# The weighted sum over the index heads of the sparse attention layer, on TensorE instead of VectorE

## The reference, cut to what matters

```
k_sel = min(TOPK_MAX, S // 4)                    # 128
dots  = einsum('bqhd,bsd->bqhs', qib, ki)        # 8 heads, 64 wide
score = einsum('bqh,bqhs->bqs', wib, relu(dots)) * IDX_DIM ** -0.5
score = where(causal, score, -inf)
_, idx = lax.top_k(score, k_sel)
```

## Time and profile before

| | |
|---|---|
| median of 3 runs | 2972.53 us (2969.16 to 2978.28) |
| the profiled execution | 2973.47 us, its span 2971.7 us |
| busy share of the span | PE 93%, DVE 54%, ACT 39% |
| index heads, from ACT's first relu to the end of the last mask | 2258.87 to 2277.71 us of the span |
| in those 18.84 us | DVE busy 15.92, PE 15.63 (with overlaps), ACT 14.02 |

### The profile page before, as it was taken

The page is one execution under the profiler, slowest core; times in us unless marked ns, Lnnn a source line. Parts: engine busy times, 40 slices in busy tenths (PEclk is TensorE's granted clock), DMA queues, the critical chain, the costliest instruction groups (busy, mean ns, idle before and its releaser), DMA issues.

```text
span 2971.7 us, 39600 instructions
## 1 busy us (share of the span) xinstructions
PE 2760.0 (93%) x15280; PEld 2328.7 (78%) x15280; DVE 1596.2 (54%) x3415; ACT 1155.1 (39%) x2524; POOL 32.0 (1%) x32
## 2 busy tenths in 40 slices
PE   7998999999999899999998989999997689899998
PEld 7888889899888787878776767888775467688886
DVE  5354656555535555555578454444566845534445
ACT  3334332433333532343334543333346354432333
POOL 1000000000000000000000000000000000000000
PEclk9998999999999999999999999999998799999999
DMA  3201212122220111212221122332221011233322
GB/s 126 77 26 41 65 37 79 54 68 87 79 75 26 59 54 48 81 57 94 89 79 47 40 68 87 97 99 93 85 71 38 20 33 43 67 100 98 100 90 89
DMA packets 115260, 205.32 MB, mean 69 GB/s; under 512 B 13824, under 2 KB 23680, under 8 KB 114944
## 3 DMA queue, kind: packets, MB, share of 16 engines
q1 hardware_dynamic: 113920, 198.60, 21.6%
q10 hardware_dynamic: 1152, 4.20, 0.4%
HBM read 200.58 MB, written 2.10 MB: 68 GB/s over the span
## 4 chain that ended last, share of the span: by engine, by line
PE 74%; DVE 15%; ACT 8%; issue 2%; DMA 0%; SPq 0%; DVEq 0%; ACTq 0%
PE pp L1985 19%; PE pp L1987 18%; PE pp L1986 18%; PE pp L2059 5%; PE pp L2035 4%; DVE wl L1552 3%; PE pp L2047 2%; ACT wh L1371 2%; PE pp L1981 1%; PE pp L1982 1%; PE pp L1983 1%; ACT P L1481 1%; DVE P L1775 1%; DVE Z L1912 1%; DVE st L1910 1%
## 5 line engine op out<-in xcount | busy, mean ns | idle before, releaser
L1985 PE MATMUL pp<-Hh,wh 128*128 128x512 f32 (+1 forms) x2304 | 866.4, 376 | 75.0 <-DVE Hl L1574 29.4
L1986 PE MATMUL pp<-Hl,wh 128*128 128x512 f32 (+1 forms) x2304 | 802.2, 348 | 0.0
L1987 PE MATMUL pp<-Hh,wl 128*128 128x512 f32 (+1 forms) x2304 | 801.2, 348 | 0.0
L1552 DVE TENSOR_TENSOR wl<-raw,wh 128x512 fp32r<-128x512 f32 (+2 forms) x774 | 499.7, 669 | 419.5 <-ACT wh L1371 405.9
L1371 ACT ACTIVATE wh<-raw 128x512 fp32r<-128x512 f32 (+2 forms) x774 | 450.7, 604 | 328.8 <-PE pp L1987 274.9
L1985 PEld LDWEIGHTS pp<-Hh,wh 128*128 128x128 f32 x2304 | 448.1, 194 | 164.1 <-DVE wl L1552 36.2
L1986 PEld LDWEIGHTS pp<-Hl,wh 128*128 128x128 f32 x2304 | 448.4, 195 | 53.8 <-issue 6.5
L1987 PEld LDWEIGHTS pp<-Hh,wl 128*128 128x128 f32 x2304 | 446.8, 194 | 52.7
L1985 PE MATMUL pp<-Yh,wh 128*128 128x512 f32 (+1 forms) x1254 | 471.8, 376 | 10.9 <-DVE Yl L1572 5.7
L1987 PE MATMUL pp<-Yh,wl 128*128 128x512 f32 (+1 forms) x1254 | 449.4, 358 | 0.0
L1986 PE MATMUL pp<-Yl,wh 128*128 128x512 f32 (+1 forms) x1254 | 449.3, 358 | 0.0
(11 more groups left out here) (242 smaller groups left out, 2632.2 us busy)
## 6 DMA issues: line engine op xcount, KB each, us to landing
raw<-in_w SPq DMA_DIRECT2D x698, 256.0 KB, 2.6
raw<-in_w SPq DMA_DIRECT2D x36, 192.0 KB, 2.3
raw<-in_w SPq DMA_DIRECT2D x40, 128.0 KB, 2.0
out<-X SPq DMA_DIRECT2D x8, 256.0 KB, 2.0
con<-in_con ACTq DMA_DIRECT2D x1, 1576.0 KB, 11.5
X<-in_x SPq DMA_DIRECT2D x2, 528.0 KB, 5.8
X<-in_x ACTq DMA_DIRECT2D x2, 528.0 KB, 6.9
Z<-in_p ACTq DMA_DIRECT2D x2, 512.0 KB, 3.3
```

The costliest lines, as they stand in the source:

```text
L1552: e.tensor_tensor(part("wl", j), landing(j), part("wh", j).bitcast(F), ALU.subtract).then_inc(*dve.up("split", j))
L1985: e.matmul(it.ps, wh, xh, start=it.first, stop=False)
L1986: e.matmul(it.ps, wh, xl, start=False, stop=False)
L1987: e.matmul(it.ps, wl, xh, start=False, stop=it.end).then_inc(*pe.up())
```

## The change

The sum over heads leaves DVE. DVE first spreads four weights at a time on diagonals: `diagonals` multiplies the 128 x 128 identity, repeated four times, by four columns of `k2`, which gives four 128 x 128 diagonal matrices side by side. There are six such instructions (24 weight columns), into three buffers in `PT` and `P`. TensorE then multiplies the relu of each head by that head's diagonal matrix, all eight heads of a block accumulating in one bank (bank 6 for i = 1 and 3, bank 5 for i = 2), in float32. DVE reads the bank once per block, adding the mask (`index total`).

The order on TensorE: heads 0, 1, 2 of the index products first, then alternately the sum of head n and the index product of head n + 3, through all 24 heads, and three sums at the end. While this runs the rotation hands out six banks (0, 1, 2, 3, 4, 7). ACT's relu now waits for TensorE's `index sum` of three heads ago where it waited for DVE.

```diff
-        relus = []
+        diagonals = [m["PT"][:, 0:512], m["PT"][:, 640:1152], m["P"][:, 0:512]]
+        spread, summed, products = {}, {}, []
+        def diagonal(n):
+            i, h = 1 + n // 2, 4 * (n % 2)
+            spread[n] = do("diagonals", to=diagonals[n % 3].rearrange("p (h d) -> p h d", h=4), ident=ident, w=k2[:, i, h:h + 4],
+                           given=summed[n - 3] if n > 2 else None, begun=indexed)["n"]
+        def add_up(i, h, bk):
+            n, x = 2 * (i - 1) + h // 4, len(products)
+            products.append((i, h))
+            ext = 128 * i + 128
+            do("index sum", ps=bank(bk)[:, 0:ext], weights=diagonals[n % 3][:, 128 * (h % 4):128 * (h % 4) + 128], spread=spread[n],
+               rl=rl[x % 3][:, 0:ext], i=i, h=h, free=free[bk] if h == 0 else None)
+            if h % 4 == 3:
+                summed[n] = (i, h)
+            if h == 7:
+                do("index total", ps=bank(bk)[:, 0:ext], i=i, mask=causal(ext), score=sel[:, i, 0:ext])
+                free[bk] = ("dve", "index total", i)
+        for n in range(3):
+            diagonal(n)
+        held.add(6)
+        rot["banks"] = [0, 1, 2, 3, 4, 7]
+        relus, wanted = [], []
         for i in range(1, 4):
             ext = 128 * i + 128
             for h in range(8):
                 bk = next_bank()
...
                 relus.append((i, h))
                 free[bk] = ("act", "index", i, h)
-            do("index_mask", score=sel[:, i, 0:ext], mask=causal(ext))
+                wanted.append((i, h, 6 if i % 2 else 5))
+                if len(wanted) > 2:
+                    add_up(*wanted.pop(0))
+                    if len(products) in (4, 8, 12):
+                        diagonal(2 + len(products) // 4)
+        for each in wanted:
+            add_up(*each)
+        held.remove(6)
+        rot["banks"] = FREE
...
     # ScalarE, index
-            act.wait_ge("dve", "index", *it.taken)
+            act.wait_ge("pe", "index sum", *it.taken)
...
     # VectorE
-    def index(it): ...
-    def index_mask(it): ...
+    def diagonals(it):
+        for other in ("act", "pe"):
+            dve.wait_ge(other, "mark", it.begun)
+        dve.wait_ge("dve")
+        if it.given:
+            dve.wait_ge("pe", "index sum", *it.given)
+        e.tensor_tensor(it.to, it.ident.unsqueeze(1).to_broadcast([128, 4, 128]), it.w.unsqueeze(2).to_broadcast([128, 4, 128]), ALU.mult)...
+    def index_total(it):
+        dve.wait_ge("pe", "index sum", it.i, 7)
+        e.tensor_tensor(it.score, it.ps, it.mask, ALU.add)...
...
     # TensorE
+    def index_sum(it):
+        if it.free:
+            pe.wait_ge(*it.free)
+        pe.wait_ge("dve", "diagonals", it.spread)
+        pe.wait_ge("act", "index", it.i, it.h)
+        e.matmul(it.ps, it.weights, it.rl, start=it.h == 0, stop=it.h == 7)...
```

More of the change, by code:

```diff
@@ L1214, in mixer_c @@
                 do("index", i=i, h=h, ps=bank(bk)[:, 0:ext], q=M[64 * (h % 2):64 * (h % 2) + 64, h, 128 * i:ext], k=(twin if h % 2 else ki)[:, 0:ext], rl=rl[n % 3][:, 0:ext], free=free[bk],
-                   indexed=indexed, taken=relus[n - 3] if n > 2 else None, scale=k2[:, i, h:h + 1], score=sel[:, i, 0:ext])
+                   indexed=indexed, taken=relus[n - 3] if n > 2 else None)
                 relus.append((i, h))
                 free[bk] = ("act", "index", i, h)
-            do("index_mask", score=sel[:, i, 0:ext], mask=causal(ext))
+                wanted.append((i, h, 6 if i % 2 else 5))
[7 more added lines that the diff above has]
+        rot["banks"] = FREE
         def rounds(i):
@@ L1892, in query_scales @@
         e.tensor_scalar(it.col[:, 0:4], it.col[:, 0:4], -it.scale, None, ALU.mult).then_inc(*dve.up())
-    def index(it):
-        dve.wait_ge("act", "index", it.i, it.h)
+    def diagonals(it):
+        for other in ("act", "pe"):
+            dve.wait_ge(other, "mark", it.begun)
         dve.wait_ge("dve")
[L1897 to L1906, removed]
+        if it.given:
+            dve.wait_ge("pe", "index sum", *it.given)
+        e.tensor_tensor(it.to, it.ident.unsqueeze(1).to_broadcast([128, 4, 128]), it.w.unsqueeze(2).to_broadcast([128, 4, 128]), ALU.mult).then_inc(
+            *dve.up("diagonals", it.n))
+    def index_total(it):
+        dve.wait_ge("pe", "index sum", it.i, 7)
+        e.tensor_tensor(it.score, it.ps, it.mask, ALU.add).then_inc(*dve.up("index total", it.i))
     def best8(it):
@@ L1928, in vector_program @@
             "turn": turn, "divide": divide, "times_z": times_z, "negs": negs, "lambda": lam, "mix": mix, "diff out": diff_out,
-            "diff norm": diff_norm, "diff scale": diff_scale, "index_key": index_key, "index_w": index_w, "query squares": query_squares, "query factors": query_factors, "query scales": query_scales, "index": index, "index_mask": index_mask,
+            "diff norm": diff_norm, "diff scale": diff_scale, "index_key": index_key, "index_w": index_w, "query squares": query_squares, "query factors": query_factors, "query scales": query_scales, "diagonals": diagonals, "index total": index_total,
             "best8": best8, "choose": choose, "mask there": mask_there}
@@ L2092, in index @@
         e.matmul(it.ps, it.q, it.k, start=True, stop=True).then_inc(*pe.up("index", it.i, it.h))
+    def index_sum(it):
[3 more added lines that the diff above has]
+        pe.wait_ge("act", "index", it.i, it.h)
+        e.matmul(it.ps, it.weights, it.rl, start=it.h == 0, stop=it.h == 7).then_inc(*pe.up("index sum", it.i, it.h))
     def mark(it):
@@ L2097, in tensor_program @@
     does = {"mark": mark, "load": load, "panel": panel, "step": step, "norm_total": norm_total, "norm_col": norm_col, "query squares": norm_col, "norm_rows": norm_rows, "rows there": rows_there, "scores": scores,
-            "turn": turn, "product": product, "turn_out": turn_out, "turn_v": turn_v, "index_w": index_w, "index": index}
+            "turn": turn, "product": product, "turn_out": turn_out, "turn_v": turn_v, "index_w": index_w, "index": index, "index sum": index_sum}
     return schedule(m, m["PP"], does)
```

## The result

The changed kernel took 3024.7 us in the median of four executions (2993.0, 3022.8, 3026.6, 3034.7); the kernel before 2972.2. The ratio is 1.0140, 95% interval 1.0105 to 1.0176. The forecast was 2993.4, range 2984 to 2999: the sign is right, the size (+52.5 us for +20.9) was off by a factor of 2.5, and one of the four executions lies where all four were expected.

What follows compares the result with a forecast made beforehand. DVE's end of the index work was taken to bound attention's start; TensorE's alternating sums and products would move it by 20.2 us, the second split adds 0.7: +20.9 on 2973.47, less 0.94 for the median, 2993.4 us, range 2984 to 2999.

Steps and rivals of the forecast that it cites:

- the first diagonals free: DVE, ahead of sum 0: the first diagonal is ready before relu 0 ends, 0.36 us of cover, so no cost.
- banks and relu buffers no bound: Index stretch: six rotating banks bring no wait; ACT's relus and three buffers do not bound pairs of 1.2 to 2.1 us.
- 4 cycles a column: TensorE float32 products and sums at 2.4 GHz: 0.43, 0.64 and 0.85 us for 256, 384 and 512 columns.
- the loss of 0.39 us per excursion to 64 rows: TensorE, 64-deep index products between 128-deep sums: 0.39 us lost each, 21 excursions, 8.2 us.
- DVE free: End of DVE's index work, after the last total: about 2297.9 against 2277.71 before, +20.2 us.
- the second split later by 0.7 us: DVE behind the index heads: second split waits for TensorE's products and ACT, 0.7 us more, between 0 and 1.2.
- Clock as the row shows, 1.00 in both stretches: TensorE's index stretch: granted clock at the upper level of 2.4 GHz, so products were costed at that pace.
- Rows 3: Profile rows before the change giving granted clock by window: 1.00 in the index stretch, 0.51 in 2279.1 to 2282.4.
- rival (c): TensorE's idle time before sum 0 lowers the clock: 1.7 us, 2995, or some 10 more, 3004; chance 0.10.
- (a): Index products alternating with sums on TensorE cost no depth switches: +12.7 us, 2985.2; chance 0.12.
- (b): Index products run beside the sums on TensorE, leaving only the sums' time: -1.3 us, 2971; chance 0.05.
- (d): DVE is late behind the index heads for another reason, the split waiting for ACT; nothing moves, 2972; chance 0.03.

Runs made afterwards that it cites:

- e2: Changed kernel with ones for the identity, so dense weights instead of diagonals (other scores): 2992.8 us profiled, the other three executions 3023.5 to 3025.9.
- e3: Changed kernel with index products over all 128 partitions, so no change of depth (other scores): median 2988.8 us, 2984 to 3006.
- e1: The changed kernel run again as it is: 3022.9 to 3026.2 us in four executions.
- e6: Changed kernel plus twelve more diagonal instructions on DVE, so TensorE idles longer ahead of sum 0: 3032.9 to 3036.9 us.
- e5: Changed kernel plus ten unread full-depth float32 products on TensorE ahead of sum 0, filling its idle time: median 2999.3 us, 2991 to 3010.
- e9: Changed kernel with e6's longer idle time and e3's index products over 128 partitions (other scores): 2998.7 to 3015.5 us.
- e10: Changed kernel with e6's longer idle time, index products and sums all 64 rows deep on partitions 0 to 63 (other scores): 3034.0 to 3035.6 us.
- e12: Changed kernel with e6's longer idle time, two true index products side by side, then two sums, eleven relu buffers: 2991.6 to 3005.5 us.
- e7: Changed kernel with only block 3 summed on TensorE, after all index products; DVE adds blocks 1 and 2: median 2969.4 us, ratio to before 0.9968.
- e8: Changed kernel with blocks 2 and 3 summed on TensorE in groups, block 1 by DVE, its picking meanwhile: median 2972.3 us, ratio to before 0.9971.
- e4: Changed kernel with twelve index products first, then four sums and four products in turn, eleven relu buffers: median 2982.7 us, 2977 to 3003.

## Why the prediction was wrong

**Right, step by step**, as e2 shows at the upper clock: the first diagonals free (sum 0 waits for the relu, not for them); banks and relu buffers no bound; 4 cycles a column (a full-depth pair of 512 columns is 1.72 us in e3, by the forecast 2 x 0.853); the loss of 0.39 us per excursion to 64 rows; DVE free at 2297.84 (2297.9); the second split later by 0.7 us (3.12 us after the first instead of 2.44, after and e2 alike); +21.2 for +20.9.

**The failed step** is the sentence "Clock as the row shows, 1.00 in both stretches". Rows 3 show the clock that other work had at those times. That PE idles ahead of sum 0 was seen and priced as rival (c), at 1.7 us, or 10 "if the gaps of the switches held the clock down for half the stretch", with 0.10. The range ended at 2999, below that 3004. What the runs showed: once the low level had set in, it lasted through the whole order in all three traces (changed, e1, e6), and the price is 69.5 - 37.6 = 31.9 us. By their times it set in in 10 of 12 executions, behind 1.7 to 2.2 us of idle time ahead of sum 0; work in place of that idle time keeps it away (e5), more idle time brings it each time (e6).

**Where (c) was mis-sized.** At 1.2 GHz the products take twice, +29.4, and an excursion costs 4.01 - 3.41 = 0.6 instead of 0.4 us, 21 times +4.2; sum 0 (0.80 us) and the last two sums of the profiled execution (1.75 us together) ran near the upper pace, which leaves the 31.9. I took the 3.3 us at 0.51 of the earlier trace rows as the length of a low phase; but in those 3.3 us TensorE ran dense products 128 rows deep, the kind of work on which e9 leaves the low level too. The weakness of the new stretch, as far as e9, e10 and e12 reach, is that half of its products fill half of the array, for want of a neighbour on the other half, which the earlier trace rows still show.

Rivals (a), (b) and (d): (a) is what e3 gives when the excursions are really taken away, +13.0 for +12.7. (b) and (d) did not occur: in e2 an index product and a sum of 512 columns follow each other in 2.11 us, their two times and not one, and the last total stands at the end of the chain.

## What to carry to other kernels

A stretch of TensorE work has two prices, one for each level of the clock, and where the order fills only half of the array the lower level may hold to its end: work out both, and put full-depth work or a pair on both halves ahead of such a stretch and into it. Moving work from DVE to TensorE paid here only in part: eight sums gave 5.0 us of distance (e7), sixteen 3.5 (e8), and all 24, grouped, cost 7.0 (e4). e7's sums were not hidden under ACT's relus either: the last relu ends at 2279.58, the total starts 4.4 us later, at 2284.01. Keep products of small depth next to their neighbour on the other half. When executions of one program differ by 1%, compare distances within the traces before explaining a median.

## What was not expected of the hardware

With TensorE's records without a gap for 69.5 us the granted clock stayed at 0.50 (e6), in e10 for 59.1 us without any change of depth, and with the changed kernel's instructions it stayed at 1.00 for 37.6 us (e2). It rose 5.5 and 4.6 us after sum 0 where products filled all rows, alone (e9) or in pairs (e12). The Trainium skill, "TensorE: Matmul & The Clock Gate", section "What's actually happening", speaks of how busy the PE has been; by their records these stretches are 100% busy, so by that reading the clock should have risen. The runs decide, and with the other half of the rows empty it did not. Leaving and entering a 64-row product cost 0.4 us at the upper level (2.11 - 1.72) and 0.6 at the lower (4.01 us against 3.41, twice the time of the full-depth pair by the forecast).
